# Rotary halves swapped by a VectorE shuffle, and eight modulation tiles moved to GpSimd

## The reference, cut to what matters

```python
def partial_rope(x, positions):              # on 16 of the 64 columns of a head
    half = ROT_DIM // 2                      # 8
    ...
    x1, x2 = xr[..., :half], xr[..., half:]
    rot = jnp.concatenate([x1 * cos - x2 * sin, x2 * cos + x1 * sin], axis=-1)
    return jnp.concatenate([rot, x[..., ROT_DIM:]], axis=-1)

# first_block, for each of two layers
    cond = jax.nn.silu(c)
    mod = (cond @ ada_w[i] + ada_b[i])       # 1024 x 6144: shifts, scales and gates
    sh1, sc1, g1, sh2, sc2, g2 = jnp.split(mod, 6, axis=-1)
    h = rmsnorm(x, norm1_g[i]) * (1.0 + sc1) + sh1
    ...                                      # layer 0: sliding window attention, 16 query heads, 2 key heads
    x = x + g1 * y
```

## Time and profile before

| | |
|---|---|
| median of 3 runs | 2267.84 us (2267.05 to 2270.59) |
| the profiled execution | 2267.9 us, its span 2265.9 us |
| TensorE busy | 2232.9 us, 99% of the span |
| VectorE, ScalarE, GpSimd busy | 1193.5 us, 895.2 us, 165.0 us |
| granted clock of the run | 0.996 |
| matmul L1006, the exchange | 9 instructions, each in 2 passes, between 61.2 and 156.3 us |
| L1590, tiles of the modulation | 70, between 55.7 and 470.4 us |

### The profile page before, as it was taken

The page is one execution under the profiler, slowest core; times in us unless marked ns, Lnnn a source line. Parts: engine busy times, 40 slices in busy tenths (PEclk is TensorE's granted clock), DMA queues, the critical chain, the costliest instruction groups (busy, mean ns, idle before and its releaser), DMA issues. The chain is left out here.

```text
span 2265.9 us, 26906 instructions
## 1 busy us (share of the span) xinstructions
PE 2232.9 (99%) x10904; PEld 1793.3 (79%) x10904; DVE 1193.5 (53%) x1651; ACT 895.2 (40%) x1445; POOL 165.0 (7%) x147
## 2 busy tenths in 40 slices
PE   8999999999999999999999999999999999999998
PEld 6766888888777778888888877887788888888886
DVE  4775755643465754333337446567752447553453
ACT  4654332223354533322333236367742224331331
POOL 2112000000000010000001001032210001000001
PEclk9999999999999999999999999999999999999999
DMA  9432555632212112232222324333333232333222
GB/s 332 149 121 84 215 212 207 215 108 93 84 57 75 57 68 94 93 103 102 94 84 98 107 75 154 103 103 112 102 114 115 84 111 85 102 94 102 93 84 84
DMA packets 82171, 258.72 MB, mean 114 GB/s; under 512 B 8800, under 2 KB 17376, under 8 KB 82048
## 3 DMA queue, kind: packets, MB, share of 16 engines
q1 hardware_dynamic: 82048, 257.01, 33.3%
HBM read 252.71 MB, written 4.26 MB: 113 GB/s over the span
## 5 line engine op out<-in xcount | busy, mean ns | idle before, releaser
L875 PE MATMUL pb<-hhi,whi 128*128 128x512 f32 x1936 | 767.3, 396 | 2.0 <-ACT hhi L1301 2.0
L877 PE MATMUL pb<-hhi,wlo 128*128 128x512 f32 x1936 | 754.3, 390 | 2.7 <-DVE wlo L1572 2.7
L879 PE MATMUL pb<-hlo,whi 128*128 128x512 f32 x1936 | 754.7, 390 | 0.0
L1572 DVE TENSOR_TENSOR wlo<-raw,whi 128x1024 fp32r<-128x1024 f32 x360 | 446.0, 1243 | 544.4 <-ACT whi L1263 544.3
L1263 ACT ACTIVATE whi<-raw 128x1024 fp32r<-128x1024 f32 x360 | 379.1, 1057 | 699.9 <-PE pb L879 675.3
L875 PEld LDWEIGHTS pb<-hhi,whi 128*128 128x128 f32 x1936 | 363.5, 188 | 88.3 <-issue 15.8
L877 PEld LDWEIGHTS pb<-hhi,wlo 128*128 128x128 f32 x1936 | 363.8, 188 | 78.9 <-DVE wlo L1572 4.1
L879 PEld LDWEIGHTS pb<-hlo,whi 128*128 128x128 f32 x1936 | 363.4, 188 | 77.9 <-DVE hlo L1669 1.3
L875 PE MATMUL pb<-ahi,whi 128*128 128x512 f32 x848 | 334.1, 394 | 1.6 <-ACT ahi L1459 0.9
L877 PE MATMUL pb<-ahi,wlo 128*128 128x512 f32 x848 | 330.2, 389 | 1.1 <-DVE wlo L1572 1.1
L879 PE MATMUL pb<-alo,whi 128*128 128x512 f32 x848 | 330.5, 390 | 0.0
(11 more groups left out here) (258 smaller groups left out, 1729.8 us busy)
## 6 DMA issues: line engine op xcount, KB each, us to landing
raw<-stream SPq DMA_DIRECT2D x360, 512.0 KB, 3.3
slab<-ada_w SPq DMA_DIRECT2D x80, 512.0 KB, 5.1
early<-ada_w SPq DMA_DIRECT2D x32, 256.0 KB, 8.1
slab<-sums SPq DMA_DIRECT2D x32, 256.0 KB, 4.2
X<-xT SPq DMA_DIRECT2D x8, 256.0 KB, 5.0
ya<-slab SPq DMA_DIRECT2D x8, 256.0 KB, 4.1
slab<-ya SPq DMA_DIRECT2D x8, 256.0 KB, 5.3
outT<-X SPq DMA_DIRECT2D x8, 256.0 KB, 2.1
```

The source lines that it names most:

```text
L875: e.matmul(out, wh, hi, start=s.k == 0, stop=False)
L877: e.matmul(out, wl, hi, start=False, stop=False)
L879: i = e.matmul(out, wh, lo, start=False, stop=s.last)
L1572: e.tensor_tensor(wlo[:, u % NW, :], raw[:, u % NRAW, :], whi[:, u % NW, :].bitcast(F), ALU.subtract).then_inc(*v_cut.up(u))
```

## The change

The exchange of the halves becomes one VectorE instruction, `stream_shuffle`, that moves rows inside each group of 32 partitions: rows 0 to 7 and 8 to 15 trade places. The tables of sines are zero in the other rows. The matmul, its PSUM bank and the constant `perm` are gone (its place in the constants stays as `room`). The eight tiles of j = 3 (n = 24 to 31) are done on GpSimd, each in two instructions: a product with the scalar, in place, and a sum (for k = 0 the product alone). A list `MOD_ORDER` gives the order of the tiles; it interleaves those of j = 3 with the first of j = 4. The sums of j = 2 are turned to columns one tile earlier.

```diff
+MOD_ORDER = [*range(16, 27), 32, 27, 33, 28, 34, 29, 35, 30, 36, 31, 37, 38, 39, *range(40, 96)]
...
     def mods():
-        for j in range(2, 12):
-            for k in range(KD):
-                if k == 3 and j in (3, 6):
-                    column_sums(j - 1)
-                tick("fma", 8 * j + k)
-                yield 1
-            if j == 7:
+        for n in MOD_ORDER:
+            j, k = divmod(n, KD)
+            if n == 26 or n == 51:
+                column_sums(2 if n == 26 else 5)
+            tick("pool_fma" if j == 3 else "fma", n)
+            yield 1
+            if n == 63:
                 column_sums(6, 7)
                 yield 1
...
-        def turn_halves(t):
-            b = take(("rope", t))
-            w.wait_ge(d_late, "in")
-            w.wait_ge(a_ev, ("qkv", qn(t) + 7 if t == "k" else t) if t != "k" else ("qkv", 8))
-            e.matmul(b, C("perm"), QG[qn(t) % 5], start=True, stop=True).then_inc(*t_att.up(("rope", t)))
-            give(("rope", t), v_att, ("rope2", t))
...
             w.wait_ge(a_ev, ("qkv", 8 if t == "k" else t))
-            e.tensor_tensor(o, g, cosT, ALU.mult).then_inc(*v_att.up(("rope1", t)))
-            w.wait_ge(t_att, ("rope", t))
             if t != "k":
                 w.wait_ge(v_att, ("rope", t - 1 if t else "k"))
-            e.tensor_tensor(qt, bank(("rope", t)), sinT, ALU.mult).then_inc(*v_att.up(("rope2", t)))
+            e.stream_shuffle(qt, g, [*range(8, 16), *range(8), *range(16, 32)]).then_inc(*v_att.up(("swap", t)))
+            e.tensor_tensor(o, g, cosT, ALU.mult).then_inc(*v_att.up(("rope1", t)))
+            w.wait_ge(v_att, ("swap", t))
+            e.tensor_tensor(qt, qt, sinT, ALU.mult).then_inc(*v_att.up(("rope2", t)))
...
+        def pool_fma(n):
+            j, k = divmod(n, KD)
+            at = MOD_ORDER.index(n) % NADA
+            a, o = ada[at], modacc[j]
+            w.wait_ge(d_ada[at], n)
+            if k == 0:
+                w.wait_ge(a_att, "cond")
+                e.tensor_scalar(o, a, cond[:, 0:1], None, ALU.mult).then_inc(*p_mod.up(("fma", n)))
+            else:
+                e.tensor_scalar(a, a, cond[:, k:k + 1], None, ALU.mult).then_inc(*p_mod.up(("scaled", n)))
+                w.wait_ge(p_mod, ("scaled", n))
+                e.tensor_tensor(o, o, a, ALU.add).then_inc(*p_mod.up(("fma", n)))
...
         def fma(n):
-            while loaded[1] < min(96, n + NADA):
+            ada_load(MOD_ORDER.index(n) + NADA)
```

More of the change, by code:

```diff
@@ L48 @@
     ("ident", 128), ("heads", 2), ("one", 1), ("invf", 32), ("sgn", 1), ("half", 8),
-    ("perm", 128), ("maskA", 256), ("maskB", 128), ("maskS", 128), ("late", 512), ("fold", 32),
+    ("room", 128), ("maskA", 256), ("maskB", 128), ("maskS", 128), ("late", 512), ("fold", 32),
 ])
@@ L207, in column_sums @@
         tick("modsum", js)
-        s.soon(3, "modrows", js)
+        s.soon(1 if js == (2,) else 3, "modrows", js)
         s.soon(7, "modturn", js)
@@ L671, in program @@
         signal(f"v_{n}") for n in ("cut", "half", "ev", "mod", "norm", "res", "att", "stick", "ssd", "conv"))
-    p_sum, p_pow, p_rope, p_ssd = (signal(f"p_{n}") for n in ("sum", "pow", "rope", "ssd"))
+    p_sum, p_pow, p_rope, p_ssd, p_mod = (signal(f"p_{n}") for n in ("sum", "pow", "rope", "ssd", "mod"))
     sums_dram = nc.dram_tensor("sums", (32, S), F, kind="Internal").ap()
@@ L1210, in tensor @@
               "tables": tables, "kstat": lambda: head_stats("k"),
-              "krope": lambda: turn_halves("k"), "kspread": kspread, "vturn": vturn, "query": query, "scores": scores, "turned": turned,
+              "kspread": kspread, "vturn": vturn, "query": query, "scores": scores, "turned": turned,
               "values": values, "start": start, "turn": turn, "gather": gather, "dtraw": dtraw, "dtsum": dtsum, "dtturn": dtturn, "xrow": xrow, "bturn": bturn,
@@ L1547, in scalar, with multiplied @@
                 do[name](*a)
+    def multiplied(n):
+        return (p_mod if n // KD == 3 else v_mod), ("fma", n)
     def item(n):
@@ L2070, in masked @@
             e.tensor_tensor(ex[:, P:], ex[:, P:], Ct[g % 2][:, P:], ALU.mult).then_inc(*p_ssd.up(("ex", g, h)))
-        do = {"angles": angles, "sine": sine, "pow": pow_, "kstat": lambda: head_pow("k"), "query": head_pow, "sq": sq,
+        do = {"angles": angles, "sine": sine, "pow": pow_, "kstat": lambda: head_pow("k"), "query": head_pow, "pool_fma": pool_fma, "sq": sq,
               "gadd": lambda i: add(("g", i // 4), i % 4), "xrow": xrow, "masked": masked}
@@ L2081, in sync @@
         w = Waits(e)
-        loaded = [0, 16]
+        loaded = [0, 0]
         def load():
@@ L2097, in fma, with ada_load @@
         def fma(n):
-            while loaded[1] < min(96, n + NADA):
-                q = loaded[1]
+            ada_load(MOD_ORDER.index(n) + NADA)
+        def ada_load(places):
+            while loaded[1] < min(len(MOD_ORDER), places):
+                place = loaded[1]
                 loaded[1] += 1
-                if q >= 16 + NADA:
-                    w.wait_ge(v_mod, ("fma", q - NADA))
-                e.dma_start(ada[(q - 16) % NADA], ada_in(q)).then_inc(*d_ada[(q - 16) % NADA].up(q))
+                q = MOD_ORDER[place]
+                if place >= NADA:
+                    w.wait_ge(*multiplied(MOD_ORDER[place - NADA]))
+                e.dma_start(ada[place % NADA], ada_in(q)).then_inc(*d_ada[place % NADA].up(q))
         def evac(tile):
@@ L2134, in final @@
             e.dma_start(io["outT"][k * P:(k + 1) * P, :], X[:, k, :]).then_inc(*d_out.up(k))
-        soon = CONST["perm"][0]
+        soon = CONST["room"][0]
         e.dma_start(cst[:, 0:soon], io["consts"][:, 0:soon]).then_inc(*d_in.up("cst"))
@@ L2149, in sync @@
         e.dma_start(cst[:, soon:], io["consts"][:, soon:]).then_inc(*d_late.up("in"))
-        fma(13)
+        ada_load(3)
         load()
         load()
-        fma(16)
+        ada_load(NADA)
         def dtgain():
@@ L2156, in dtgain @@
             e.dma_start(wdt, io["wdt"]).then_inc(*d_wdt.up("in"))
-        do = {"dtgain": dtgain, "lower": lambda u: load() if u > 2 else None, "fma": fma, "evac": evac, "dtturn": dtturn, "decay": lambda g, h: row(8 * g + h + 1), "fetch": fetch, "final": final}
+        do = {"dtgain": dtgain, "lower": lambda u: load() if u > 2 else None, "fma": fma, "pool_fma": fma, "evac": evac, "dtturn": dtturn, "decay": lambda g, h: row(8 * g + h + 1), "fetch": fetch, "final": final}
         for name, *a in ticks:
```

15 lines of the change are left out of this document (4 added, 11 removed).

## The result

Runs side by side: 2278.56 us after (median of 6, 2277.3 to 2280.99), 2269.14 us before (median of 6, 2267.05 to 2272.43). The ratio is 1.004, with a 95% interval of 1.003 to 1.005: slower by 9.4 us, where 2.4 were predicted. The profiled execution took 2278.19 us, its span 2276.3, which is 10.4 more than before.

What follows compares the result with a forecast made beforehand. TensorE was taken as the bound, busy 99% of the span. Stalls of 9.2 us less a gain of 6.8 us gave +2.4 on 2267.9, so 2270.3 us; range 2261 to 2275, the forecast's own 2266 to 2274.

Steps and rivals of the forecast that it cites:

- Without any side effect this is 5.2 + 0.6 + 1.0 = 6.8 us: Attention gain: 5.2 us from exchange matmuls removed at t = 1 to 5, 0.6 and 1.0 from shorter waits for maxima.
- The other edits cost nothing: Column-sum matmuls only trade places, and SyncE's buffer refill waits for GpSimd tiles in time: no cost.
- The product at 1.2 us: GpSimd's product with the scalar, 1024 columns: 1.2 us, bounds 1.2 and 2.4.
- The power: GpSimd's power ahead of each tile takes 2.0 us, so the tile's product follows it and waits for rope's last sum.
- So a VectorE instruction with two SBUF operands waits until GpSimd's instruction is over: Shared SBUF port pair is an exclusive lock for a whole instruction, delaying VectorE however small its instruction.
- six were forecast: Sign: L1831, behind the maxima, takes 2.4 instead of 0.17 us in six of its 16 instances.
- The stall of 3.1 us at t = 2: Two GpSimd tiles in a row hold VectorE's copy, so TensorE stands 3.1 us; bounds 0.8 and 3.1.
- about 0: Stall of TensorE at t = 3: slack of 3 us covers the tile's cost of 0.6 + 2.3, so about 0.
- 0.84 for 1.7: At t = 5, TensorE was to stall 1.7 us, with 0.4 more for a bank of the output projection.
- The sum of stalls: TensorE stalls from GpSimd locking VectorE in the attention: 3.1 + 0.9 + 2.1 + 1.2 + 1.9 = 9.2 us.
- The shuffle: The stream_shuffle in rope takes 0.6 us in VectorE's queue, bounds 0.4 and 1.3.
- the rival built on it: Shuffle holds VectorE 1.3 instead of 0.6 us, adding 4.9 us on the path: 2275.2 us; chance 15%.

Runs made afterwards that it cites:

- f1_fill: Kernel before with only the shuffle replacing the exchange, plus four unused extra matmuls ahead of the product with the values of t = 4 and 5: 2266.26 us.
- s3: Changed kernel with all tiles on VectorE, none on GpSimd, keeping the new order of tiles and column sums: 2271.66 us, ratio 1.0013.
- s1: Kernel before with the exchange done by the shuffle and nothing else changed: 2269.26 us, ratio 1.0000.
- s2: Changed kernel with the exchange still on TensorE as before; GpSimd tiles and new order kept: 2278.12 us, ratio 1.0041.
- l1: Changed kernel with GpSimd's seven sums left out, so the vector of j = 3 is not summed up; products stay: 2270.12 us, ratio 1.0001.
- l4: Changed kernel with GpSimd's tiles, except the one with k = 0, held back until behind the maxima's two small instructions: 2271.20 us, ratio 1.0006.
- l3: Changed kernel with every GpSimd tile but the first (k = 0) cut into pieces of 256 columns: 2268.43 us, ratio 0.9994.
- p1: Changed kernel with GpSimd tiles in 256-column pieces, plus unused extra matmuls ahead of the values of t = 4 (four) and 5 (three): 2267.03 us, ratio 0.9988.

## Why the prediction was wrong

The steps, with what the parts add up to: the median of before beside the result lies 1.3 us above the 2267.84 that the prediction started from; 2269.1 - 0.1 (shuffle) + 2.4 (order) + 6.9 (GpSimd) = 2278.3. The parts are steps of one chain of runs, so their sum had to come out; their sizes are what the runs tell.

- **"Without any side effect this is 5.2 + 0.6 + 1.0 = 6.8 us"** is the step that failed most. The shuffle alone gives 0.1 where the removed matmuls were to give 5.2. TensorE does run ahead, by 3.26 us at t = 6 (not 5.2, mainly because it is 0.6 late at L998 of t = 1, and at t = 5 the scores wait 0.59 us for rope). I added up savings ahead of a wait, and took the waits at t = 6 and 7 as neutral. But a lead is worth only what the chain that ends the wait has gained too, and that chain, on VectorE, got longer by the shuffle. 1.0 and 0.6 of the sum were counted on a tile leaving that chain, so they belong to the part on GpSimd.
- **The clock** was not in the prediction at all. The lead turned into idle time, and the granted clock fell behind it; `f1_fill` shows 3.0 us of that. The trace of before had such waits of 1.1 us with a clock of 1.00 behind them, and I didn't ask what 2.9 us would do. The Trainium skill (TensorE: Matmul & The Clock Gate, "HAM oscillation — how this bites in real kernels") describes this for waits on DMA: the matmuls behind such waits run slow. The trace agrees for a wait on VectorE, with 0.63 for 0.39 us.
- **"The other edits cost nothing"** was wrong by 2.4 us (`s3` against `s1`). I looked at where the column sums' matmuls stand, and not at who takes their bank later. Without the exchange's bank and with the sums one iteration earlier, it falls to the scores of (4, 0), and its reader L1606 is 4.6 us late for them. With the exchange's bank kept it falls to the product with the values and costs 3.4 us there (`s2`). The sum's lock makes up half of that wait (`l1`).
- **The product at 1.2 us** was mis-sized: 2.85. The bound of 2.4, the sum's time, was not high enough either. The power was mis-sized too: taken at 2.0 us from the trace of before, it took 1.65 beside the shuffle. So GpSimd's product, taken to start behind rope, started 0.15 us ahead of rope's last sum and stopped it.
- **"So a VectorE instruction with two SBUF operands waits until GpSimd's instruction is over"** is right for the sum: L1831 took 2.15 to 2.25 us in seven of its 16 instances, where six were forecast. That it met the sum was luck, though. With the product at its true length the sum starts 4.8 us behind the statistics and not 4.0, and L1831, due at 4.0 by the prediction, would have passed ahead of it; it came late by the 0.8 us that the product cost rope. In `s2`, where that didn't happen, it passed each time. For the product it is wrong: L1799, issued 0.15 into it, ends 1.66 behind its start, so with its own 0.69 it was held for 0.97 us; L1852 in `l4` gives the same, 1.39 - 0.43 = 0.96. The rule of the Trainium skill that was cited (SBUF — State Buffer, "Who interferes with whom"), a lock held for a whole instruction, fits the sum only; here the measurement decides.
- **The stall of 3.1 us at t = 2** was 1.55. A copy is held too (1.22 for 0.43 in `l4`), but in the changed kernel it came 1.48 us into the product, and went through in 0.43. At t = 3 it was 0.80 and 0.75 us for "about 0", at t = 5 0.84 for 1.7.
- **The sum of stalls**, 9.2 us, less the 1.6 for tiles that leave VectorE's chain, is 7.6 and stands against the 6.9 us that GpSimd costs by `s3`. The total came close, while its terms were off in both directions, so the closeness is luck in part. With the removed matmuls at 5.2 and the order at nothing, GpSimd's 6.9 would have made the kernel 1.7 us slower, near the 2.4 forecast.
- **The shuffle** at 0.6 in the queue was right, and the rival built on it fell. L1014 stayed at 66.40 (66.15 before), as said.

## What to carry to other kernels

Work taken from the busiest engine counts only up to its next wait: ask whether the chain that ends that wait gets shorter too, and if it gets longer, expect the lead to become idle time that costs the clock a second time. When a bank leaves the rotation or a `take` moves, write down who gets every bank afterwards and whether its reader is late. Work for GpSimd beside a VectorE that works on SBUF goes in small pieces (256 columns here: 10.1 us of 2278.6, lock and timing together), or behind the critical instructions (7.4 us). When an instruction is expected to meet another, write down by how much: here 0.13 us decided which one was locked.

## What the runs showed of the hardware

- A product with a scalar per partition on GpSimd took longer than a sum of two tensors: 2.85 against 2.36 us at 128x1024, and 0.96 against 0.70 at 128x256 (3.82 and 2.80 for four).
- At 128x1024 the product held VectorE's two operand instructions for its first 0.97 us only: issued 1.2 us or more into it, they took their usual time (L1842 in `s2`). A copy of 128x512 was held for the first 0.96 us (`l4`), went freely when issued 1.48 us into the product, and was held again when issued at 1.94 to 2.29 us, until 2.7 us (`s2`, all six: 0.83 to 1.19 us instead of 0.43). The sum held two operand instructions for its whole length.
- GpSimd's power beside a shuffle took 1.64 us (139.69 in `s1`), beside VectorE's product 2.01.
- The granted clock behind a wait of 2.5 us was 1.00 in one run (118 to 121 us in `l3`) and 0.50 in another (`p1`); behind one of 2.12 us it was 0.56 (`l1`, 118 to 121 us). So a wait of this length has no fixed price.
